# Value product with V stationary in two column halves, and reciprocal sums spread by a product with the identity

## The chip, the cores and the metric

The kernel runs on one core of a Trainium2 chip. The metric is device time in microseconds for one execution, the median of several runs. A core has TensorE (matmul; its weight loads are shown apart), VectorE, ScalarE, GpSimd and the DMA queues, each with its own list of instructions, tied together by semaphores only. In the rows PE is TensorE, PEld its weight loads, DVE VectorE, ACT ScalarE, POOL GpSimd.

## The reference

Two transformer layers on 512 tokens of width 1024. Layer 0 mixes with sliding-window attention (16 query heads, 4 key-value heads, window 128, a learned sink per head), layer 1 with a forgetting attention over all earlier keys. After each comes a router with the same mixture of 16 experts. What the change touches is the attention of both layers:

```python
# layer 0: keys of the block before and of the own block; a sink logit in the softmax
probs = jax.nn.softmax(jnp.concatenate([scores, sink_col], axis=-1), axis=-1)[..., :-1]
out = jnp.einsum('bnhgqs,bnshd->bnqhgd', probs.astype(vv.dtype), vv)
return out.reshape(B, S, SWA_Q_HEADS * HEAD_DIM) @ w_o
# layer 1: all keys up to the own block
p = jax.nn.softmax(jnp.where(causal, s, NEG), axis=-1)
outs.append(jnp.einsum('bhqk,bkhd->bqhd', p.astype(v.dtype), v[:, :end]))
```

Everything is float32. The output projection needs the attention output with the model dimension on partitions, in two parts, attn_high and attn_low, whose sum is the float32 value.

## The kernel before

Layer 0 runs its input projection, then attention, output projection, normalisation, router, experts; layer 1 the same. Attention works on pairs of heads (hp, eight per layer), and for each pair on four blocks of 128 queries in the order 0, 3, 1, 2 (`N_ORDER`). A pair and a block is a step s, 32 steps per layer. In layer 0 block 0 has one key block and the others two; in layer 1 block n has n + 1. So a pair has 7 key blocks in layer 0 and 10 in layer 1.

One step, for both heads ("halves") of the pair:

- TensorE, `scores(s)`: Q times K, two matmuls of 64 rows each, one head in each row half of the array. In layer 1 a bf16 matmul adds the causal mask (L548).
- VectorE, `mask_and_max(s, half)`: bias, and the row's maximum, from PSUM to the buffer sp (L1091 in layer 0, L1098 in layer 1).
- ScalarE, `expo(s, half)`: exponentials and row sums (L807).
- TensorE, `turn_probs(s)`: 128x128 transposes of the probabilities, head 0 to bank 3, head 1 to bank 4 (L559).
- ScalarE copies head 0's from PSUM to the buffer pT (`evac_probs`, L821), VectorE head 1's (L1115). There is one pT for each head, so a copy waits for the product of the step before (pv_done), and the next transposes for the copy.
- TensorE, `mix(s)`: the product with V (L576). Stationary is a 128x128 block of pT, moving are 64 columns of V; the result has queries on partitions. It goes to bank 5 or 6, by the parity of hp, first all of head 0, then all of head 1.

After a pair's four steps VectorE's `normalise(hp)` takes reciprocals of the row sums (L1123 adds the sinks in layer 0, L1126) and divides the bank into heads_out (L1130). TensorE's `turn_out(hp)` turns that into the same bank with four transposes (L584), ScalarE's `out_high_part` casts it to attn_high (L832), and VectorE's `evac_out` makes attn_low (L1137). ScalarE also casts the output weights in the odd steps (L827).

The order on each engine is the order of the code. TensorE's loop is, for each s:

```python
turn_probs(s)
if s >= 1: mix(s - 1)
if s + 2 < STEPS: scores(s + 2)
if s >= NT and s % NT == 1: turn_out(s // NT - 1)
```

VectorE's is copy of step s, masks of step s + 2, then in the first step of the next pair `normalise`, in its third `evac_out`. ScalarE's is exponentials of step s + 1 for head 0, copy of step s, exponentials of step s + 1 for head 1, then the rest. The output projection follows; its matmuls are lines L454 to L456, 21 of them before it needs the last pair.

## Time and profile before

| | us |
|---|---|
| median of 3 runs | 1023.93 (1016.85 to 1025.27) |
| the profiled execution | 1014.57 |
| its span, first to last instruction | 1012.4 |
| layer 0's attention | about 90 to 160 |
| layer 1's attention | about 604 to 691 |
| TensorE busy, share of the span | 879.1, 87% |
| VectorE, ScalarE, GpSimd busy | 385.4, 249.5, 122.5 |

"Busy" is the union of an engine's instructions. Matmuls overlap, so the duration of a row of matmul is longer than its distance to the next row; what counts is the distance from start to start, or the time that the chain of waits gives to a group. A float32 matmul of the code is two rows of MATMUL and two of LDWEIGHTS; a transpose is one. A form such as `64*128` is the part of the array, rows and columns; `128x64` behind it is the size of the moving operand.

### The profile page before, as it was taken

To read this page: it belongs to the slowest core of one execution; us is meant where nothing else is said; L and a number is where in the kernel's file an instruction comes from. 1 tells how busy PE (TensorE), PEld (TensorE's weight loads), DVE (VectorE), ACT (ScalarE), POOL (GpSimd) and SP (SyncE) were. 2 spreads that over 40 slices of the span, in tenths; PEclk is the share of its full clock that TensorE was granted. 3 is DMA by queue.
4 is the path that set the end of the run, shared out by engine and by line. 5 is a ranking of instruction groups with operands and counts; after the bars stand their busy time and mean duration, and the time that the engine had idled before them with its cause. 6 is when DMAs were issued, how large, how long until landed. Compare 5 with 4: busy or idle time off the path is not lost.

```text
span 1012.4 us, 10845 instructions
## 1 busy us (share of the span) xinstructions
PE 879.1 (87%) x3900; PEld 561.4 (55%) x3900; DVE 385.4 (38%) x928; ACT 249.5 (25%) x605; POOL 122.5 (12%) x137
## 2 busy tenths in 40 slices
PE   6999999966899999918999999999975899999910
PEld 5887777852344444306878877877862344444300
DVE  3534884444111111157332226663445111111137
ACT  3323882000121111041222227772000121111100
POOL 2001331113000000032000002221113000000024
PEclk9999999978999999958999999999977899999965
DMA  9996100068699999644162232111059499999234
GB/s 324 339 353 213 48 1 1 1 233 314 178 356 345 351 354 321 213 133 153 63 209 83 84 111 98 43 43 42 1 179 347 135 352 358 351 342 327 93 115 166
DMA packets 110286, 196.69 MB, mean 194 GB/s; under 512 B 6608, under 2 KB 72144, under 8 KB 110240
## 3 DMA queue, kind: packets, MB, share of 16 engines
q1 hardware_dynamic: 92864, 132.34, 38.0%
q0 software_dynamic: 10432, 39.36, 11.6%
q10 hardware_dynamic: 6944, 24.38, 7.4%
q8 instruction: 28, 0.46, 0.2%
q14 instruction: 18, 0.15, 0.0%
HBM read 158.81 MB, written 37.26 MB: 194 GB/s over the span
## 4 chain that ended last, share of the span: by engine, by line
PE 81%; DVE 8%; DMA 4%; POOL 3%; issue 2%; ACT 1%; POOLq 0%; SPq 0%; DVEq 0%; ACTq 0%
PE bank L649 21%; PE bank L661 11%; PE bank L454 10%; PE bank L456 10%; PE bank L455 10%; PE bank L576 5%; PE bank L542 4%; PE bank L559 3%; PE bank L643 2%; PE bank L440 2%; PE bank L611 1%; POOL xs L406 1%; DMA arena<-ys,pos 1%; POOL veps L366 1%; DVE xres L987 1%
## 5 line engine op out<-in xcount | busy, mean ns | idle before, releaser
L649 PE MATMUL bank<-ring,arena 128*96 128x512 f32 x512 | 228.6, 600 | 2.8 <-issue 1.4
L649 PEld LDWEIGHTS bank<-ring,arena 128*96 128x96 f32 x512 | 84.2, 165 | 140.1 <-issue 138.3
L661 PE MATMUL bank<-ring,arena 128*96 128x512 f32 x256 | 116.4, 597 | 2.7 <-DVE arena L1268 2.7
L1268 DVE COPY arena<-bank 128x192 f32<-128x192 f32 x32 | 11.4, 357 | 194.9 <-PE bank L654 194.9
L454 PE MATMUL bank<-high,x_high 128*128 128x512 f32 x160 | 67.1, 419 | 10.5 <-DVE low L993 5.4
L807 ACT ACTIVATE arena<-arena,nmax 128x256 f32<-128x256 f32 (+3 forms) x128 | 66.9, 522 | 31.1 <-DVE nmax L1098 19.9
L661 PEld LDWEIGHTS bank<-ring,arena 128*96 128x96 f32 x256 | 39.1, 162 | 55.3 <-issue 51.1
L576 PE MATMUL bank<-arena 128*128 128x64 f32 x544 | 68.1, 269 | 0.2 <-ACT arena L821 0.2
L576 PEld LDWEIGHTS bank<-arena 128*128 128x128 f32 x544 | 65.8, 192 | 0.5 <-ACT arena L821 0.5
L421 POOL DMA_INDIRECT arena<-ys,pos x16 | 19.5, 1220 | 382.8 <-issue 382.8
L455 PE MATMUL bank<-low,x_high 128*128 128x512 f32 x160 | 65.2, 408 | 0.0
L456 PE MATMUL bank<-high,xlow 128*128 128x512 f32 x160 | 64.8, 405 | 0.0
L393 POOL TENSOR_TENSOR low<-ring,high 128x512 fp32r<-128x512 f32 x32 | 40.6, 1270 | 181.9 <-ACT high L827 181.9
L1278 DVE COPY arena<-bank 96x512 f32<-96x512 f32 x32 | 22.0, 687 | 97.9 <-PE bank L661 97.9
L871 ACT ACTIVATE arena<-bank 96x256 f32<-96x256 f32 x32 | 12.1, 379 | 184.6 <-PE bank L649 184.6
L454 PE MATMUL bank<-high,attn_high 128*128 128x512 f32 x128 | 51.8, 405 | 0.0
L456 PE MATMUL bank<-high,attn_low 128*128 128x512 f32 x128 | 51.2, 400 | 0.0
L455 PE MATMUL bank<-low,attn_high 128*128 128x512 f32 x128 | 51.0, 398 | 0.0
L456 PE MATMUL bank<-x_high,wsplit 128*128 128x512 f32 x128 | 50.6, 395 | 0.0
L454 PE MATMUL bank<-x_high,wsplit 128*128 128x512 f32 x128 | 50.2, 392 | 0.0
L455 PE MATMUL bank<-xlow,wsplit 128*128 128x512 f32 x128 | 49.9, 390 | 0.0
L440 PE MATMUL bank<-ident,xres 128*128 128x128 f32 x128 | 20.8, 316 | 32.1 <-DVE xres L987 27.8
(200 smaller groups left out, 1222.2 us busy)
## 6 DMA issues: line engine op xcount, KB each, us to landing
ring<-in_w_gate SPq DMA_DIRECT2D x32, 1024.0 KB, 7.0
ring<-in_w_up SPq DMA_DIRECT2D x32, 1024.0 KB, 9.6
ring<-in_w_down SPq DMA_DIRECT2D x32, 1024.0 KB, 12.7
ys<-arena ACTq DMA_DIRECT2D x32, 384.0 KB, 6.6
ring<-in_fox_w_in SPq DMA_DIRECT2D x6, 2048.0 KB, 9.3
arena<-xs ACTq DMA_DIRECT2D x30, 384.0 KB, 6.5
xs<-lnp POOLq DMA_DIRECT2D x1, 9984.0 KB, 43.8
ring<-in_swa_w_in SPq DMA_DIRECT2D x3, 2048.0 KB, 12.3
```

The lines of the kernel that those rows point to most:

```text
L393: eng.tensor_tensor(low, w, high, ALU.subtract).then_inc(S(f"out_low{l}"), 1)
L440: mm = eng.transpose(bank[3 + c // 4][:, (c % 4) * P:(c % 4 + 1) * P], xres[:, t, c * P:(c + 1) * P], ident[:, :])
L454: eng.matmul(out, ah, wh, start=(c == 0), stop=False)
L455: eng.matmul(out, ah, wl, start=False, stop=False)
L456: return eng.matmul(out, al, wh, start=False, stop=(c == KC - 1))
L542: mm = eng.matmul(s_bank(s, half)[:, 0:nk], QT[r, hp, n * P:(n + 1) * P], KT[r, kp, k0 * P:k1 * P], start=True, stop=(l == 0))
L559: mm = eng.transpose(bank[3 + half][:, i * P:(i + 1) * P], sp[:, 2 * (s % 2) + half, i * P:(i + 1) * P], ident[:, :])
L576: mm = eng.matmul(bank[5 + hp % 2][:, at:at + HD], pT[:, half, i * P:(i + 1) * P], (V0 if l == 0 else V)[:, k0 + i, v:v + HD], start=(i == ...
L649: mm = eng.matmul(bank[2 + b][0:CAP, :], xeT[:, b, c, :], w[:, c, :], start=(c == 0), stop=(c == KC - 1))
L661: mm = eng.matmul(bank[5 + half][0:CAP, :], hT[:, b, c, :], w[:, c, half * BLK:(half + 1) * BLK], start=(c == 0), stop=(c == FC - 1))
L807: eng.activation(p, p, ACT.Exp, bias=nmax[:, hp % 2, n, half:half + 1], scale=-1.0, accum_out=rsum[:, hp % 2, n, half:half + 1]).then_inc( ...
L1278: eng.tensor_copy(ysb[0:CAP, b, BLK:D], bank[6][0:CAP, :]).then_inc(S(f"y_dve{l}"), 1)
```

## The change

The product is turned round: the 64 columns of V of a head are stationary, 128 columns of pT are moving, and the result has the head's dimension on partitions, already the layout that the output projection wants. Head 0 goes to the left column half of the array and partitions 0 to 63 of bank 5, head 1 to the other half and partitions 64 to 127. The matmuls of the two heads alternate, and both need their pT at the start. The output transposes are gone.

The division now needs the reciprocals along the free dimension: `sums(hp)` on VectorE computes them at the end of the pair's last step, `spread_sums(hp)` on TensorE multiplies them, spread over 64 columns as the stationary operand, with the identity into bank 6 (8 matmuls, 16 rows), `evac_shares(hp)` on ScalarE copies that to heads_out, and `divide(hp)` on VectorE multiplies bank 5 by it. Cast and subtraction then read heads_out in SBUF instead of PSUM. Every pair uses bank 5 for the product and bank 6 for the spread; the first product of a pair waits for o_ready of the pair before, where it waited for aT_ready of two pairs before.

```diff
--- before.py
+++ after.py
@@ -564,25 +564,33 @@
                     hp, n = STEP[s]
                     k0, k1 = keys(n)
                     if s % NT == 0:
-                        if hp >= 2:
-                            eng.wait_ge(S("aT_ready"), PAIRS * l + hp - 1)
+                        if hp >= 1:
+                            eng.wait_ge(S("o_ready"), PAIRS * l + hp)
                         elif l == 0:
-                            eng.wait_ge(S("qkT_free"), GROUPS[0] - 1 + hp)
-                    for half in range(2):
-                        eng.wait_ge(S(f"pT_ready{half}"), STEPS * l + s + 1)
-                        v = HD * (2 * hp // (NH // NKV) if l == 0 else 2 * hp + half)
-                        at = HD * (2 * n + half)
-                        for i in range(k1 - k0):
-                            mm = eng.matmul(bank[5 + hp % 2][:, at:at + HD], pT[:, half, i * P:(i + 1) * P],
-                                            (V0 if l == 0 else V)[:, k0 + i, v:v + HD], start=(i == 0), stop=(i == k1 - k0 - 1))
-                        mm.then_inc(S("pv_done"), 1)
-
-                def turn_out(hp):
-
-                    eng.wait_ge(S("o_ready"), PAIRS * l + hp + 1)
+                            eng.wait_ge(S("qkT_free"), GROUPS[0])
+                    for i in range(k1 - k0):
+                        for half in range(2):
+                            if i == 0:
+                                eng.wait_ge(S(f"pT_ready{half}"), STEPS * l + s + 1)
+                            v = HD * (2 * hp // (NH // NKV) if l == 0 else 2 * hp + half)
+                            mm = eng.matmul(bank[5][HD * half:HD * half + HD, n * P:(n + 1) * P],
+                                            (V0 if l == 0 else V)[:, k0 + i, v:v + HD], pT[:, half, i * P:(i + 1) * P],
+                                            start=(i == 0), stop=(i == k1 - k0 - 1))
+                            if i == k1 - k0 - 1:
+                                mm.then_inc(S("pv_done"), 1)
+
+                def spread_sums(hp):
+
+                    eng.wait_ge(S("sums_ready"), PAIRS * l + hp + 1)
+                    if hp >= 1:
+                        eng.wait_ge(S("shares_here"), PAIRS * l + hp)
                     for n in range(NT):
-                        mm = eng.transpose(bank[5 + hp % 2][:, n * P:(n + 1) * P], heads_out[:, hp % 2, n * P:(n + 1) * P], ident[:, :])
-                    mm.then_inc(S("oT_done"), 1)
+                        for half in range(2):
+                            mm = eng.matmul(bank[6][HD * half:HD * half + HD, n * P:(n + 1) * P],
+                                            rinv[:, hp % 2, n, half:half + 1].to_broadcast([P, HD]), ident[:, :],
+                                            start=True, stop=True)
+                            if n == NT - 1:
+                                mm.then_inc(S("spread"), 1)
 
                 if l == 0:
                     eng.wait_ge(S("consts"), 1)
@@ -594,12 +602,12 @@
                     turn_probs(s)
                     if s >= 1:
                         mix(s - 1)
+                    if s >= NT and s % NT == 0:
+                        spread_sums(s // NT - 1)
                     if s + 2 < STEPS:
                         scores(s + 2)
-                    if s >= NT and s % NT == 1:
-                        turn_out(s // NT - 1)
                 mix(STEPS - 1)
-                turn_out(PAIRS - 1)
+                spread_sums(PAIRS - 1)
 
 
                 def route(t):
@@ -802,7 +810,7 @@
                     nk = P * (min(n, 1) + 1) if l == 0 else P * (n + 1)
                     eng.wait_ge(S("sp_ready"), 2 * STEPS * l + 2 * s + half + 1)
                     if s >= 2 * NT and s % NT == 0 and half == 0:
-                        eng.wait_ge(S("o_ready"), PAIRS * l + hp - 1)
+                        eng.wait_ge(S("sums_ready"), PAIRS * l + hp - 1)
                     p = sp[:, 2 * (s % 2) + half, 0:nk]
                     eng.activation(p, p, ACT.Exp, bias=nmax[:, hp % 2, n, half:half + 1], scale=-1.0,
                                    accum_out=rsum[:, hp % 2, n, half:half + 1]).then_inc(S("exp_done"), 1)
@@ -826,10 +834,17 @@
                     weights_here(eng, OUT_USE[l] + p // KC)
                     eng.copy(high, w).then_inc(S(f"out_high{l}"), 1)
 
+                def evac_shares(hp):
+
+                    eng.wait_ge(S("spread"), 2 * (PAIRS * l + hp + 1))
+                    if hp >= 2:
+                        eng.wait_ge(S("aT_ready"), PAIRS * l + hp - 1)
+                    eng.copy(heads_out[:, hp % 2, :], bank[6][:, :]).then_inc(S("shares_here"), 1)
+
                 def out_high_part(hp):
 
-                    eng.wait_ge(S("oT_done"), PAIRS * l + hp + 1)
-                    eng.copy(attn_high[:, hp, :], bank[5 + hp % 2][:, :]).then_inc(S("aT_high"), 1)
+                    eng.wait_ge(S("o_ready"), PAIRS * l + hp + 1)
+                    eng.copy(attn_high[:, hp, :], heads_out[:, hp % 2, :]).then_inc(S("aT_high"), 1)
 
                 expo(0, 0)
                 expo(0, 1)
@@ -843,8 +858,11 @@
                         expo_sinks(s // NT)
                     if s % 2 == 1:
                         out_weights_high(s // 2)
-                    if s >= NT and s % NT == 2:
+                    if s >= NT and s % NT == 0:
+                        evac_shares(s // NT - 1)
+                    if s >= NT and s % NT == 1:
                         out_high_part(s // NT - 1)
+                evac_shares(PAIRS - 1)
                 out_high_part(PAIRS - 1)
 
                 for t in range(NT):
@@ -1114,7 +1132,7 @@
                         eng.wait_ge(S("pv_done"), 2 * STEPS * l + 2 * (s - 1) + 2)
                     eng.tensor_copy(pT[:, 1, 0:nk], bank[4][:, 0:nk]).then_inc(S("pT_ready1"), 1)
 
-                def normalise(hp):
+                def sums(hp):
 
                     eng.wait_ge(S("exp_done"), 2 * STEPS * l + 2 * NT * (hp + 1))
                     rs = rsum[:, hp % 2, :, :]
@@ -1122,19 +1140,19 @@
                         eng.wait_ge(S("sink_exp"), hp + 1)
                         link(eng.tensor_tensor(esink[:, hp % 2, :, :], esink[:, hp % 2, :, :], rs, ALU.add))
                         rs = esink[:, hp % 2, :, :]
-                    ri = rinv[:, hp % 2, :, :]
-                    link(eng.reciprocal(ri, rs))
-                    eng.wait_ge(S("pv_done"), 2 * STEPS * l + 2 * NT * (hp + 1))
                     if hp >= 2:
-                        eng.wait_ge(S("oT_done"), PAIRS * l + hp - 1)
-                    eng.tensor_tensor(heads_out[:, hp % 2, :].rearrange("p (n h d) -> p n h d", n=NT, h=2),
-                                      bank[5 + hp % 2][:, :].rearrange("p (n h d) -> p n h d", n=NT, h=2),
-                                      ri.unsqueeze(3).to_broadcast([P, NT, 2, HD]), ALU.mult).then_inc(S("o_ready"), 1)
+                        eng.wait_ge(S("spread"), 2 * (PAIRS * l + hp - 1))
+                    eng.reciprocal(rinv[:, hp % 2, :, :], rs).then_inc(S("sums_ready"), 1)
+
+                def divide(hp):
+
+                    eng.wait_ge(S("shares_here"), PAIRS * l + hp + 1)
+                    eng.tensor_tensor(heads_out[:, hp % 2, :], bank[5][:, :], heads_out[:, hp % 2, :], ALU.mult).then_inc(S("o_ready"), 1)
 
                 def evac_out(hp):
 
                     eng.wait_ge(S("aT_high"), PAIRS * l + hp + 1)
-                    eng.tensor_tensor(attn_low[:, hp, :], bank[5 + hp % 2][:, :],
+                    eng.tensor_tensor(attn_low[:, hp, :], heads_out[:, hp % 2, :],
                                       attn_high[:, hp, :], ALU.subtract).then_inc(S("aT_ready"), 1)
 
                 if l == 0:
@@ -1151,11 +1169,13 @@
                             mask_and_max(s + 2, half)
                     if l == 0 and s % NT == 1:
                         shift_sinks(s // NT)
+                    if s % NT == NT - 1:
+                        sums(s // NT)
                     if s >= NT and s % NT == 0:
-                        normalise(s // NT - 1)
+                        divide(s // NT - 1)
                     if s >= NT and s % NT == 2:
                         evac_out(s // NT - 1)
-                normalise(PAIRS - 1)
+                divide(PAIRS - 1)
                 evac_out(PAIRS - 1)
```

On TensorE, at the step in which a pair of layer 0 ends (L576 is the product, L542 scores, L559 transposes of probabilities, L584 the old output transposes, L589 the new product with the identity), before:

```order
L559 MATMUL bank<-ident,arena 128x128 x2
L576 MATMUL bank<-arena 128x64 x4
L542 MATMUL bank<-arena 128x256 x2
L559 MATMUL bank<-ident,arena 128x128 x4
L576 MATMUL bank<-arena 128x64 x2
L542 MATMUL bank<-arena 128x256 x2
L584 MATMUL bank<-ident,arena 128x128 x4
```

and now:

```order
L559 MATMUL bank<-ident,arena 128x128 x2
L576 MATMUL bank<-arena 64x128 x4
L589 MATMUL bank<-ident,rinv 64x128 x8
L542 MATMUL bank<-arena 128x256 x2
L559 MATMUL bank<-ident,arena 128x128 x4
L576 MATMUL bank<-arena 64x128 x2
L542 MATMUL bank<-arena 128x256 x2
```

The spread stands ahead of the scores that VectorE's next masks need, and the product behind the next transposes is the first of the new pair.

On VectorE at the same place (L1115 copies probabilities, L1091 masks, L1123 and L1126 make the reciprocals, L1130 divides; in the new file L1133, L1109, L1141, L1145 and L1150), before:

```order
L1115 COPY arena<-bank 128x128 [waits pv_done,pT_done]
L1091 ISA arena,nmax<-bank,band,sink 128x256 [waits pT_done,s_done]
L1091 ISA nmax 128x1
L1091 ISA arena,nmax<-bank,band,sink 128x256 [waits pT_done,s_done]
L1091 ISA nmax 128x1
L1123 TENSOR_TENSOR esink<-esink,rsum 128x8 [waits sink_exp,exp_done]
L1126 RECIPROCAL rinv<-esink 128x8 [waits dve_step]
L1130 TENSOR_TENSOR arena<-bank,rinv 128x512 [waits oT_done,pv_done,dve_step]
L1115 COPY arena<-bank 128x256 [waits pv_done,pT_done]
```

and now:

```order
L1141 TENSOR_TENSOR esink<-esink,rsum 128x8 [waits sink_exp,exp_done]
L1145 RECIPROCAL rinv<-esink 128x8 [waits spread,dve_step]
L1133 COPY arena<-bank 128x128 [waits pv_done,pT_done]
L1109 ISA arena,nmax<-bank,band,sink 128x256 [waits pT_done,s_done]
L1109 ISA nmax 128x1
L1109 ISA arena,nmax<-bank,band,sink 128x256 [waits pT_done,s_done]
L1109 ISA nmax 128x1
L1150 TENSOR_TENSOR arena<-bank,arena 128x512 [waits shares_here]
L1133 COPY arena<-bank 128x256 [waits pv_done,pT_done]
```

The reciprocals moved ahead of the copy and the masks, one step earlier; the division kept its place behind the masks and now waits for ScalarE's copy.

## Rows read from the trace of the kernel before

**Rows 1.** Stretches: us; busy us of PE, PEld, DVE, ACT, POOL; clock; DMA; GB/s.
```profile
90.00:163.00 73.00, 67.44 (x508) 53.73 (x507) 56.61 (x204) 54.71 (x192) 21.43 (x18) 1.00 0.16 52
605.00:692.00 87.00, 85.81 (x698) 68.92 (x696) 54.18 (x182) 62.66 (x183) 22.92 (x22) 1.00 0.19 61
```

**Rows 2.** Timeline, layer 0's products: start us, us, engine, line, operands, form, rows.
```profile
112.58 1.00 PE L576 MATMUL bank<-arena 128*128 128x64 f32 x8
...
114.50 1.00 PE L576 MATMUL bank<-arena 128*128 128x64 f32 x8
...
116.35 1.00 PE L576 MATMUL bank<-arena 128*128 128x64 f32 x8
...
118.40 0.56 PE L576 MATMUL bank<-arena 128*128 128x64 f32 x4
...
120.94 0.45 PE L576 MATMUL bank<-arena 128*128 128x64 f32 x3
```

**Rows 3.** Chain of waits, one pair of layer 1: start us, us, what.
```profile
622.32 1.73 PE bank L576 x16
...
625.36 0.84 PE bank L576 x8
626.20 1.06 PE bank L542 x4
...
627.70 1.29 PE bank L576 x12
...
630.72 0.39 PE bank L576 x4
...
633.05 1.73 PE bank L576 x16
```

**Rows 4.** Timeline of layer 0, the ring through ScalarE; in brackets idle time and releaser.
```profile
115.15 0.37 ACT L821 COPY arena<-bank 128x256 f32<-128x256 f32 x1
115.42 0.40 ACT L807 ACTIVATE arena<-arena,nmax 128x128 f32<-128x128 f32 x1
...
116.07 0.22 PEld L559 LDWEIGHTS bank<-ident,arena 128*128 128x128 f32 x2 [0.33 <-ACT arena L807]
```

**Rows 5.** Score rows running at 615.5 us: duration ns min/median/max, first and last start.
```profile
L542 PE MATMUL bank<-arena x2: 693/693/693, 615.4 to 615.4; 64*128 64x512 f32 x2
```

**Rows 6.** Timeline of layer 1, from product to scores to the masks' end.
```profile
617.92 0.19 PEld L576 LDWEIGHTS bank<-arena 128*128 128x128 f32 x1
...
618.18 0.30 PEld L542 LDWEIGHTS bank<-arena 64*128 64x128 f32 x4
...
619.78 0.20 DVE L1126 RECIPROCAL rinv<-rsum 128x8 f32<-128x8 f32 x1
```

**Rows 7.** Timeline of TensorE at the forget gate's projection.
```profile
509.04 0.40 PE L456 MATMUL bank<-high,xlow 128*128 128x512 f32 x1
509.27 0.40 PE L454 MATMUL bank<-x_high,wf_parts 128*16 128x512 f32 x1
```

**Rows 8.** Timeline of layer 0 at the end of a pair.
```profile
117.28 0.70 PE L542 MATMUL bank<-arena 64*128 64x256 f32 x4
...
118.83 0.16 DVE L1123 TENSOR_TENSOR esink<-esink,rsum 128x8 f32<-128x8 f32 x1
...
119.26 0.69 DVE L1130 TENSOR_TENSOR arena<-bank,rinv 128x512 f32<-128x512 f32 x1
...
120.01 0.66 PE L584 MATMUL bank<-ident,arena 128*128 128x128 f32 x4 [0.42 <-DVE arena L1130]
```

**Rows 9.** Masks by form: rows, busy us, mean ns of one, idle before.
```profile
L1091 DVE CUSTOM_DVE_ANT_0 arena<-bank,band,sink 128x256 f32<-128x256 f32 x47 | 20.9, 481 | 3.0 <-PE bank L542 1.9
...
L1098 DVE CUSTOM_DVE_ANT_0 arena<-bank,lnp 128x512 f32<-128x512 f32 x16 | 10.4, 689 | 4.9 <-PE bank L548 4.9
```

**Rows 10.** Stretches at the end of layer 1's attention, columns as in the first group.
```profile
690.10:693.50 3.40, 2.38 (x21) 2.11 (x20) 1.36 (x3) 1.00 (x2) 2.29 (x3) 1.00 0.03 5
693.50:696.90 3.40, 3.40 (x11) 2.75 (x9) 0.69 (x1) 0.59 (x1) 0.00 (x1) 0.50 0.92 270
```

## The prediction

> **What bounds the kernel now.** I read the two attention stages, since the change touches nothing else: first the table of stretches, then the timeline and the chain of waits, product by product. In the table [rows 1] layer 0's attention has TensorE busy 67 of 73 us and layer 1's 86 of 87, both at the full granted clock. One pair of heads is four steps, in the order of query blocks 0, 3, 1, 2. From one product of block 3 to the next, layer 0 takes 120.94 - 112.58 = 8.36 us [rows 2] and layer 1 633.05 - 622.32 = 10.73 us [rows 3]. The intervals that begin with the products of blocks 3, 1, 2 and 0 are 1.92, 1.85, 2.05 and 2.54 us in layer 0, and 3.04, 2.34, 3.02 and 2.33 us in layer 1. In layer 1 the chain is TensorE alone, so there fewer TensorE nanoseconds would count. Layer 0 is a ring, and the reader should see in [rows 4] that a transpose waited 0.33 us for ScalarE: a product starts (114.50), ScalarE copies the next step's probabilities for head 0 (115.15) and does the exponentials of the step after it for head 1 (115.42), TensorE transposes those (116.07), and the next product starts (116.35).
>
> **The product itself.** Each product of the code shows as two rows of matmul. Now 16 rows take 1.73 us in the chain, 0.108 us each [rows 3]. Afterwards a row loads 64 columns and streams 128. No row of before has that form. From the scores, full fp32 products too: two rows of 512 columns, one after the other, lie in 1.06 us with their first load, less 0.2 us for load and change of shape, so 0.43 us for 512 columns and 0.107 us for 128 [rows 3]. I take 0.11 us. Whether the two heads run side by side decides the rest. The scores' row halves do: two rows start at 615.4 together and last 693 ns each [rows 5], and four rows of 0.43 us of work take 1.06 us, not 1.7 [rows 3]. I take the same for column halves, since those rows are nearest: 2 x 0.11 us per key block for both heads, 4 x 0.11 now. A pair has 7 key blocks in layer 0 (1.54 us saved) and 10 in layer 1 (2.2 us saved). The other end, no overlap, saves nothing and is kept for the range.
>
> An entry into the halves may cost something. From a full product to the scores, weight loads stand 618.18 - 617.92 = 0.26 us apart [rows 6] where two rows of a product stand 0.11 apart: 0.15 us for that change. But the step from `128*128` to `128*16` costs nothing: 509.04 to 509.27 is the usual 0.23 us of such matmuls [rows 7]. That shape narrows columns, as the new products do, so I take 0.05 us per step (a first load no longer hidden) and keep 0 and 0.15 as ends. The Trainium skill (TensorEngine Tiling, Key Properties) says that changing the tiling mode drains TensorE. The row on `64*128` agrees, the one on `128*16` does not; by the rule alone some 63 further entries would add up to 63 x 0.15 = 9 us, part of it inside the waits below.
>
> **Why layer 0 gains little.** Its ring does not wait for the whole product but for head 0's part, and that is now the first 4 of 8 rows. The new order alternates the heads, so head 0 is done only with the fourth pair: 4 row times again. The 0.65 us from product to ScalarE's copy [rows 4] stay. So the intervals from blocks 1 and 0 become 1.85 and 1.8 us; the one from block 3 becomes 2.2, because the cast to attn_high moves to that step, next to a weight cast on ScalarE.
>
> **The new wait.** All pairs now accumulate in bank 5, so block 0's product of the next pair waits for o_ready, the end of `divide`. From the start of block 2's product, layer 0:
> the product, 4 x 0.11 = 0.44;
> `spread_sums` waits for the reciprocals, which stand on VectorE behind a copy and two masks: after the copy 2 x 0.48 [rows 9], some 0.1 of it overlapped, and 0.4 for sum and reciprocal (118.83 to 119.26 [rows 8]), 1.2 to 1.3 in all, where TensorE needs about 0.8 for transposes and product: 0.4 exposed;
> 16 rows of the product with the identity, in pairs: 8 x 0.11 = 0.88;
> change of shape 0.15, and the scores to the end of the second mask, 117.28 to 118.83 = 1.55 [rows 8];
> `divide`, queued behind those masks, 0.69 [rows 8] and two wakings of 0.04.
> Sum 4.2 us against 2.05. ScalarE's copy of the shares, no longer than the 0.69 of a 512-column pass, lies beside scores and masks and costs nothing; if the division moved ahead of the masks, it would. The four output transposes go, 0.66 us behind 0.42 us of waiting for the old division [rows 8]: that is most of 2.54 - 1.8. The next step's `evac_probs` is queued behind `divide` on VectorE, and ScalarE's waits for the product after it, so nothing fills the hole.
> One pair of layer 0: 2.2 + 1.85 + 4.2 + 1.8 = 10.05 us against 8.36, **+1.7**.
>
> Layer 1, the same walk: product 6 x 0.11 = 0.66; the masks are 512 wide and take 2 x 0.69 [rows 9], so the reciprocals come about 0.7 late; spread 0.88; change 0.15; scores to the end of the second mask, 619.78 - 618.18 = 1.6 [rows 6]; division and wakings 0.77. Sum 4.75 us against 3.02. The other three shrink until ScalarE's ring binds. From block 3: 0.88 until head 0 is done, 0.2 to the copy, 0.3 copy, 0.7 exponentials and read-out, 0.4 transposes, 0.1 waking and entry: 2.6. From blocks 0 and 1, 2.0 each, where TensorE's own transposes and scores of 384 and 512 columns stand. Pair: 11.4 against 10.73, **+0.7**.
>
> At the end of each stage a spread of 0.88 us stands before the output projection, in place of a division of 0.69, its wakings and 0.66 us of transposes [rows 8]: -0.6 each. The copies and the division behind it (about 2.9 us) lie beside 21 matmuls of 0.23 us in the projection's first group (4.9 us).
>
> Sum over seven intervals a layer: 7 x 1.7 - 0.6 + 7 x 0.7 - 0.6 = 11.3 + 4.3 = **+15.6 us**. The profiled execution took 1014.57 us (span 1012.4, and 2.2 around it); the median of the runs shown is 1023.93, 9.4 above it. The sum gives 1030.2 beside the first and 1039.5 beside the second. I predict **1039**.
>
> **The rivals.**
> *The wait is covered, and it is faster* (0.06). Place: block 0's product behind `divide`. If spread to o_ready took no more than TensorE's own scores and transposes (about 1.9 us in layer 1, 1.3 in layer 0), TensorE would bind layer 1: -2.2 for the product, +0.88 - 0.44 for spread against transposes, +0.2 for entries, -1.5 a pair, and layer 0's ring at 1.8 a step gives 7.2 against 8.36. Eight pairs: -12 - 9, 1003. Against it: `divide` stands behind both masks, which gives 2.5 us.
> *Gain and wait balance* (0.16). The reciprocals come in time (0.4 and 0.7 us) and each step's ring runs 0.1 us shorter: -0.8 and -1.1 a pair, -15 in all, 1024.
> *The column halves do not overlap* (0.11), so the change does not do what it says. Then 14 and 20 more row times a pair and 8 more for the spread, at most 2.4 and 3.1 us a pair, 44 in all; some falls into the waits, so about 1072; half an overlap gives 1055. For it speaks that no row here has two column halves.
> *The clock falls* (0.10). Before layer 1's projection TensorE was busy 2.38 of 3.40 us, and the next stretch ran at a granted 0.50, 1.2 GHz [rows 10]; layer 0's stage with 0.92 busy kept 1.00 [rows 1]. The new holes of over 1 us bring layer 0 nearer to the former. A stretch at half clock costs about 1 us; eight to twelve of them give 1050. The Trainium skill (TensorE: Matmul & The Clock Gate, Part 1) calls the throttled state the default that activity releases; the rows agree.
>
> **Numbers.** The forecast has 0.57 and holds 1030 to 1048 by itself (entries at 0 or 0.15 us, reciprocals earlier or later, layer 1's steps 0.1 off). To 0.8 the range takes in most of the balance and the clock, and half an overlap: **1023 to 1062**. 1%, 10 us, is about what a measurement can tell here from no change. Faster by over 1%: 0.06. Within 1%: 0.16 and the lowest tenth of the forecast, 0.21. Slower: 0.73.
>
> **What the new profile would show.** Right: rows that load 64 columns start in twos, 0.11 us between twos; block 0's product waits for VectorE's division, over 1 us in layer 0 and some 0.7 in layer 1; pairs of 10.0 and 11.4 us; a lower busy share of TensorE in both stages; nothing moved elsewhere. Wrong: the division starts before the masks end, or ScalarE's copy of the shares ends last; product rows start one by one; the granted clock leaves 1.00 inside a stage; the spread never waits for the reciprocals.

## The result and the profile after

| | before | after |
|---|---|---|
| median, us | 1021.49 (4 runs, 1016.85 to 1025.27) | 1038.04 (4 runs, 1029.61 to 1038.62) |
| profiled execution, its span, us | 1014.57, 1012.4 | 1029.61, 1027.8 |
| layer 0's attention, first scores to output projection, us | 70.73 | 87.75 |
| layer 1's attention, us | 88.88 | 93.16 |
| product to product, layer 0, intervals from blocks 3, 1, 2, 0, us | 1.93, 1.84, 2.06, 2.53 | 2.29, 1.82, 5.17, 1.82 |
| the same, layer 1, us | 3.03, 2.34, 3.02, 2.34 | 2.69, 2.09, 4.67, 2.03 |

The change made the kernel slower: ratio 1.0145, 95% interval 1.0074 to 1.0216. A pair takes 11.10 us in layer 0 (8.36 before) and 11.48 us in layer 1 (10.73 before). Two of layer 0's pairs have 4.04 and 4.09 us where the others have 5.17; that difference is what the forecast did not have at all. Stage times and intervals here come from the profiled executions, which were 7 and 8 us shorter than the two medians; where those microseconds lie no trace shows.

The table of stretches after answers to [rows 1] (columns as there; the third row is a stretch at the end of layer 0's attention):

```profile
90.00:176.00 86.00, 67.72 (x587) 40.72 (x588) 63.03 (x200) 58.58 (x198) 21.40 (x18) 0.99 0.14 44
620.00:710.00 90.00, 81.95 (x764) 50.76 (x764) 52.44 (x180) 64.39 (x188) 22.18 (x21) 1.00 0.19 60
...
174.00:177.50 3.50, 3.50 (x26) 3.00 (x25) 0.44 (x2) 0.85 (x2) 1.27 (x1) 0.52 0.03 7
```

TensorE is as long busy in layer 0 as before (67.7 against 67.4 us) in a stage that is 17 us longer; in layer 1 it has 8 us of holes in 90, where it had 1.2 in 87. The clock holds but for one stretch of 3.5 us.

The timeline of layer 0 after, over one end of a pair and the beginning of the next, answers to [rows 2, 4, 8]. L1141 adds the sinks, L1145 is the reciprocal, L589 the spread, L1150 the division, L393 GpSimd's subtraction for the low part of the output weights:

```profile
118.25 0.66 PE L576 MATMUL bank<-arena 128*64 128x128 f32 x8
...
120.06 0.66 PE L576 MATMUL bank<-arena 128*64 128x128 f32 x8
...
120.34 1.27 POOL L393 TENSOR_TENSOR low<-ring,high 128x512 fp32r<-128x512 f32 x1 [2.95 <-ACT high L835]
...
120.38 1.25 DVE L1141 TENSOR_TENSOR esink<-esink,rsum 128x8 f32<-128x8 f32 x1
...
121.66 0.20 DVE L1145 RECIPROCAL rinv<-esink 128x8 f32<-128x8 f32 x1
...
121.92 1.09 PE L589 MATMUL bank<-ident,rinv 128*64 128x128 f32 x16 [1.20 <-DVE rinv L1145]
...
122.94 0.70 PE L542 MATMUL bank<-arena 64*128 64x256 f32 x4
...
124.49 0.69 DVE L1150 TENSOR_TENSOR arena<-bank,arena 128x512 f32<-128x512 f32 x1
...
125.23 0.44 PE L576 MATMUL bank<-arena 128*64 128x128 f32 x4 [1.00 <-DVE arena L1150]
...
129.34 0.66 PE L576 MATMUL bank<-arena 128*64 128x128 f32 x8
...
131.20 0.66 PE L576 MATMUL bank<-arena 128*64 128x128 f32 x8
...
131.47 1.30 POOL L393 TENSOR_TENSOR low<-ring,high 128x512 fp32r<-128x512 f32 x1 [2.98 <-ACT high L835]
...
131.47 0.17 DVE L1141 TENSOR_TENSOR esink<-esink,rsum 128x8 f32<-128x8 f32 x1
```

Read it downwards. `[1.20 <-DVE rinv L1145]` means that the engine stood idle for 1.20 us until that instruction of VectorE released it. The last product of the pair starts at 120.06. The sum of eight elements behind the masks, 0.16 us in [rows 8], takes 1.25 us here: it begins 0.04 us after GpSimd's subtraction and ends with it. The spread waits for the reciprocals behind it. The scores come after the spread, the masks after the scores, the division after the masks, and the next product after the division, 5.17 us after the last. At 131.47 the same sum starts together with the subtraction and takes 0.17 us: this is one of the two pairs with 4.1 us.

The chain of waits in layer 1 after, at the same place (answers to [rows 3, 6]):

```profile
644.43 0.13 DVE rinv L1145
...
644.60 1.09 PE bank L589 x16
645.69 0.63 PE bank L542 x4
...
647.30 0.61 DVE arena L1150
...
647.96 0.44 PE bank L576 x4
...
650.06 1.02 PE bank L576 x16
```

The product of 16 rows takes 1.02 us where it took 1.73, and the chain leaves TensorE twice in a pair, for the reciprocals and for the division, where it had been TensorE alone.

What the product and the spread waited for, over the whole program:

```profile
L576 PE MATMUL bank<-arena x544: 272/273/417, 93.3 to 712.1; 128*64 128x128 f32 x182
...
  DVE arena L1150: 24.8, 28
```
```profile
L589 PE MATMUL bank<-ident,rinv x256: 272/273/417, 99.7 to 712.9; 128*64 128x128 f32 x128
...
  DVE rinv L1145: 21.6, 26
```

These sums count TensorE's matmuls and its weight loads apart (28 waits are 14 pairs, each seen twice). The matmuls alone stood 1.00 us a pair for the division in layer 0 and 0.54 in layer 1, and 1.20 us for the reciprocals in the five held pairs of layer 0 and 0.43 in layer 1.

### The profile page after: what moved, and what is told of

It reads as the page before. It is cut to its first block, busy times and chain, and to the rows that moved or that the text cites. A ratio compares the mean times of both kernels' runs of the same rounds, so it can differ in the third digit from the quotient of the medians.

```text
span 1027.8 us, 11268 instructions
## 1 busy us (share of the span) xinstructions
PE 881.2 (86%) x4092; PEld 533.6 (52%) x4092; DVE 392.8 (38%) x928; ACT 258.1 (25%) x621; POOL 122.6 (12%) x137
## 4 chain that ended last, share of the span: by engine, by line
PE 77%; DVE 10%; DMA 4%; issue 3%; POOL 3%; ACT 2%; POOLq 0%; DVEq 0%; SPq 0%
PE bank L657 20%; PE bank L669 11%; PE bank L454 10%; PE bank L456 10%; PE bank L455 10%; PE bank L542 3%; PE bank L576 3%; PE bank L559 2%; PE bank L651 2%; PE bank L589 2%; PE bank L440 2%; PE bank L619 1%; POOL xs L406 1%; DMA arena<-ys,pos 1%; DMA xs<-xres,pos 1%
## 5 line engine op out<-in xcount | busy, mean ns | idle before, releaser
L393 POOL TENSOR_TENSOR low<-ring,high 128x512 fp32r<-128x512 f32 x32 | 40.6, 1272 | 203.2 <-ACT high L835 203.1
L559 PE MATMUL bank<-ident,arena 128*128 128x128 f32 x272 | 50.1, 287 | 5.9 <-ACT arena L829 4.9
L576 PE MATMUL bank<-arena 128*64 128x128 f32 x544 | 44.4, 286 | 11.9 <-DVE arena L1150 10.7
```

The source lines that it names most:

```text
L393: eng.tensor_tensor(low, w, high, ALU.subtract).then_inc(S(f"out_low{l}"), 1)
L559: mm = eng.transpose(bank[3 + half][:, i * P:(i + 1) * P], sp[:, 2 * (s % 2) + half, i * P:(i + 1) * P], ident[:, :])
L576: mm = eng.matmul(bank[5][HD * half:HD * half + HD, n * P:(n + 1) * P], (V0 if l == 0 else V)[:, k0 + i, v:v + HD], pT[:, half, i * P:(i + ...
```

## The experiments

Each ratio, with its 95% interval, is to the kernel before, run beside it (medians 1015.15 to 1016.13 us). The changed kernel was not run again beside them, so its 1038.04 us comes from other runs than theirs; the intervals of the traces compare it more closely. Pairs are read from product to product. Edits are against the changed kernel, unless it says otherwise.

**GpSimd's subtraction in four pieces.** Is VectorE's sum held by the subtraction that runs beside it?

```diff
-eng.tensor_tensor(low, w, high, ALU.subtract).then_inc(...)
+for q in range(4):
+    c = slice(q * P, (q + 1) * P)
+    ins = eng.tensor_tensor(low[:, c], w[:, c], high[:, c], ALU.subtract)
+ins.then_inc(...)
```

> The changed kernel with GpSimd's subtraction of the output weights (L393, 1.27 us) cut into four pieces of 128 columns. Theory (a VectorE instruction with two SBUF inputs stands still while GpSimd works in SBUF): the 1.25 us rows of the sum of sinks and exponentials (L1141, 5 of 8 in layer 0) fall to 0.6 us or less, and the interval from block 2's product to block 0's in layer 0, 5.17 us in five pairs and 4.04 to 4.09 in the rest, is below 4.5 everywhere; layer 0's attention, 87.75 us, loses 4 to 5 us, layer 1's 93.16 stays within 0.5. Rival (the 1.25 us are VectorE's own, or a lock held over all of GpSimd's work): nothing changes. Total 1034 against 1038.

```profile
119.35 1.69 POOL L395 TENSOR_TENSOR low<-ring,high 128x128 fp32r<-128x128 f32 x4 [2.51 <-ACT high L838]
...
119.39 0.43 DVE L1144 TENSOR_TENSOR esink<-esink,rsum 128x8 f32<-128x8 f32 x1
...
123.43 0.44 PE L579 MATMUL bank<-arena 128*64 128x128 f32 x4 [1.00 <-DVE arena L1153]
```

The sum takes 0.43 us, the length of a piece, not of the whole. The interval goes from 5.17 to 4.36 us in the same five pairs, layer 0's attention from 87.75 to 82.63 us, layer 1 stays at 11.48 a pair. The hold is shown, and its length is that of the GpSimd instruction in progress. The total does not show the gain: 1033.72 us, ratio 1.0186 (1.0133 to 1.024), and a profiled span of 1027.7 us against 1027.8, because the two stages of experts, which no edit touches, took 198.3 and 198.6 us in this execution against 195.5 each.

**The two heads in turn** (all matmuls of head 0, then all of head 1). Does the alternating order cost the early release of head 0?

```diff
-for i in range(k1 - k0):
-    for half in range(2):
+for half in range(2):
+    for i in range(k1 - k0):
```

> The changed kernel with the product's rows of head 0 first and then those of head 1, so that the two column halves cannot run side by side. Theory (layer 0 is a ring that waits for head 0's rows only): in layer 0 the intervals from blocks 3, 1 and 0 stay at 2.29, 1.82 and 1.82 within 0.1, that from block 2 grows by about 0.4; layer 1, whose products are longer, loses about 0.3 to 0.9 an interval, some 2 us a pair: 94 grows to about 109. Rival (the saving of the overlap was what carried the change in both layers): each layer-0 interval grows by about 0.4, 1.6 us a pair, 12 us. If the halves did not overlap in the changed kernel either, nothing changes.

```profile
119.95 0.66 PE L576 MATMUL bank<-arena 128*64 128x128 f32 x8
```

Eight rows take the same 0.66 us as in the alternating order: the halves run side by side although the program names them one after the other. Only the product of 16 rows is longer, 1.31 us from first to last start against 0.82. Pairs are 11.1 and 11.6 us (layer 0's first took 13.9, with its sum held for 2.93 us); 1036.17 us in 2 runs, 1.0207 (1.0138 to 1.0276). So the expectation failed: this order does not take the overlap away, and layer 1 lost 0.1 us a pair, not 2. Head 0's last row starts only 13 ns before head 1's, so the order of the code can't win the early release back either.

**The kernel before with one late signal** (an edit of the kernel before: head 0's product signals only when head 1's is done).

```diff
-    mm.then_inc(S("pv_done"), 1)   # after each half
+mm.then_inc(S("pv_done"), 2)       # after both
```

> The kernel before, with one difference: head 0's product does not signal its end; both are signalled with head 1's. Theory (the ring of layer 0 lives on the early signal of head 0): ScalarE's copy comes 4 rows, 0.44 us, later, so the intervals of layer 0 grow from 1.93, 1.84 and 2.06 to about 2.3 each and a pair from 8.36 to about 9.5, +9 us; in layer 1, bound by TensorE, a pair grows from 10.73 by less than 1 us. Rival (TensorE binds layer 0 too): both stages keep their times within 2 us.

```profile
121.40 0.85 PE bank L576 x8
...
122.33 0.38 ACT arena L821
```

ScalarE's copy now follows the end of the product in the chain. Pairs: 8.97 us in layer 0 (+0.61, where about 1.1 was expected) and 11.15 in layer 1 (+0.42); 1025.61 us, 1.0095 (1.005 to 1.0141). The early release of head 0 is real, at 0.6 us a pair in layer 0. In the new form head 0 ends only with the whole product, so a product that is shorter by half releases it no sooner.

**Two banks in turn** for product and spread, as the kernel before had them, so that no product waits for the division of the pair just ended.

```diff
-eng.wait_ge(S("o_ready"), PAIRS * l + hp)          # mix
+eng.wait_ge(S("shares_here"), PAIRS * l + hp)
-... bank[5][HD * half:..., n * P:(n + 1) * P]       # product
+... bank[5 + hp % 2][HD * half:..., n * P:(n + 1) * P]
-... bank[6][HD * half:..., n * P:(n + 1) * P]       # spread, and ScalarE's copy of it
+... bank[6 - hp % 2][HD * half:..., n * P:(n + 1) * P]
-eng.wait_ge(S("shares_here"), PAIRS * l + hp)      # spread
+eng.wait_ge(S("o_ready"), PAIRS * l + hp)
-... bank[5][:, :]                                  # what divide reads
+... bank[5 + hp % 2][:, :]
```

> The changed kernel with the pairs alternating between banks 5 and 6, the spread going to the bank of the next pair; block 0's product then waits for ScalarE's copy of the shares and not for the division. Theory (the new wait of block 0's product on the division, 1.0 us in layer 0 and 0.5 to 0.7 in layer 1): the interval from block 2 to block 0 falls by 1.0 in layer 0 and 0.6 in layer 1, 8 + 5 = 13 us if nothing else takes its place; total about 1026. Rival (VectorE's order holds the ring anyway, since its copy for the next step stands behind the division): the wait moves to the transposes after it and the pair keeps its 10 to 11 us: gain below 4 us.

```profile
643.03 0.13 DVE rinv L1145
...
643.20 1.09 PE bank L589 x16
644.30 0.63 PE bank L542 x4
644.93 0.22 PE bank L548 x2
645.15 0.88 PE bank L559 x8
646.03 0.37 PE bank L576 x4
```

Behind the spread the chain of layer 1 is TensorE alone; the wait for the reciprocals is left. The long interval goes from 4.67 to 4.06 us in layer 1, from 5.17 to 4.09 in layer 0 (2.97 in the pair whose sum is not held). Layer 0's first interval of the kind took 7.28 us: its sum was held for 2.57 us, through two subtractions in a row, and from 100.9 us on TensorE ran for 10.2 us at a granted 0.50. 1021.64 us, 1.0049 (1.0018 to 1.008).

**The division ahead of the masks**, banks as in the change: the other way to free the bank earlier.

```diff
+if s >= NT and s % NT == 0: divide(s // NT - 1)   # now ahead of mask_and_max
-if s >= NT and s % NT == 0: divide(s // NT - 1)   # was behind it
```

> The changed kernel with the division ahead of the two masks on VectorE in the step in which it falls, not behind them. Theory (block 0's product waits for the division behind scores and masks, 2.5 us from the spread's end; ahead of them it would wait 0.2 for the spread's end, 0.6 for ScalarE's copy of the shares, 0.7 for the division, 1.6 in all, while TensorE does scores and transposes in 1.3 and 1.8): the interval from block 2 to block 0 falls by about 0.9 in layer 0 (5.17 to 4.3) and 0.7 in layer 1 (4.67 to 4.0). The masks then come up to 0.8 later, so the intervals behind may give back some 0.2. Rival (ScalarE reaches the copy of the shares only behind its exponentials, and the masks held up hold those): less than 0.3 falls.

Layer 1's interval is 4.06 us, the same as with two banks. In layer 0 it is 4.38, and the one after it grows from 1.82 to 2.16, since the masks now start later: the pair is 10.65 us against 11.10. 1028.37 us, 1.011 (1.0079 to 1.0141). The masks ahead of the division are what the bank's wait is made of, and moving the division only hands part of that wait on in layer 0.

**The reciprocals ahead of the masks**, banks as in the change.

```diff
+if s % NT == NT - 1: sums(s // NT)   # now ahead of mask_and_max(s + 2)
-if s % NT == NT - 1: sums(s // NT)   # was behind it
```

> The changed kernel with the reciprocals of a pair ahead of the two masks of its last step on VectorE, not behind them. Theory (the spread waits for them, 1.2 us in layer 0 where the sum with the sinks stands still behind GpSimd, 0.4 to 0.6 in layer 1): the interval from block 2 to block 0 falls from 5.17 to about 4.0 or less in layer 0 and from 4.67 to about 4.2 in layer 1, since the masks then come 0.4 us later and are hidden behind the spread: 9 + 4 us, total about 1026. Rival (the masks behind them set the division's time, so the wait only moves): the interval from block 2 stays within 0.3 and the total within 4 us of the changed kernel's 1038.

```profile
646.90 0.81 PE bank L576 x12
647.70 0.87 PE bank L589 x16
648.58 0.63 PE bank L542 x4
```

The spread follows the product without a wait. The interval is 4.02 us in layer 1 (-0.65). In layer 0 it is 3.75 in every pair: -0.33 against the undisturbed pairs, and the 1.08 of the hold gone too, because the sum now runs before the subtraction starts. 1018.75 us, 1.0024 (0.9995 to 1.0053): this one move brings the median to where it can't be told from before, though the profiled attention stages (78.86 and 88.59 us) are still 7.8 us longer than before's.

**Both heads in one column half.** The head 1 part goes to the left half too, into bank 6, so the columns that it should fill lie elsewhere, the output is wrong, the router sees other values, and the total (1373.83 us) is not comparable: layer 1's experts took 523 us, where the kernel has an extra loop for tokens beyond an expert's places. Only the attention stages are compared.

```diff
-mm = eng.matmul(bank[5][HD * half:HD * half + HD, n * P:(n + 1) * P],
+mm = eng.matmul(bank[5 + half][0:HD, n * P:(n + 1) * P],
```

> The changed kernel with both heads' products in the left column half (head 1's into bank 6, so its output columns are not the reference's): the row halves of the array stay as they are, only the running side by side is taken away. Theory (side by side is worth one row time of 0.11 us for each two rows, but the ring of layer 0 waits for head 0 only): a 16-row product lasts 1.8 us instead of 1.02, an 8-row product 0.9 instead of 0.59. Rows alternate, so head 0 now ends with the last row but one: intervals of layer 0 grow by 0.4 (blocks 3 and 1) and 0.2 (block 0), a pair by 1.3, 10 us; in layer 1 by 0.2, 0.9, 0.4 and 0.6, a pair by 2.1, 17 us; total about 1065. Rival (the queue already serialises them): nothing changes.

First and last start of the eight rows of one product, in this kernel and then in the changed one (columns as in [rows 5]):

```profile
L576 PE MATMUL bank<-arena x8: 272/273/323, 120.6 to 121.4; 128*64 128x128 f32 x8
```
```profile
L576 PE MATMUL bank<-arena x8: 272/273/323, 120.1 to 120.4; 128*64 128x128 f32 x8
```

Rows stand 109 ns apart one by one (160 ns after the first); in the changed kernel they start in twos, 6 to 7 ns apart, with the same distances from two to two. A pair is 11.3 us in layer 0 (+0.2, where 1.3 was expected) and 12.62 in layer 1 (+1.14, where 2.1 was). The column halves do run side by side. In layer 0 that is worth next to nothing while the waits stand.

**All repairs together**: two banks, reciprocals ahead of the masks, the subtraction in pieces, and the cast to attn_high one step later (`s % NT == 2` where it was `== 1`), away from the weight cast.

> The changed kernel with alternating banks 5 and 6, reciprocals ahead of the masks, GpSimd's subtraction in four pieces, and the cast to attn_high in the pair's third step as before. Theory (all of the loss lies in the new waits and one crowded step of ScalarE): layer 0's intervals from blocks 3, 1, 2, 0 become 1.95, 1.82, 3.2, 1.82, a pair 8.8 against 8.37 before; layer 1's 2.65, 2.1, 3.6, 2.0, a pair 10.35 against 10.73. Attention 75 and 86 us against 70.7 and 88.9 before: total within 3 us of the kernel before. Rival (other waits take their place): pairs above 9.5 and 11 us, total above 1025.

Pairs: 2.04 + 1.82 + 2.68 + 1.83 = 8.36 us in layer 0 and 2.69 + 2.09 + 3.41 + 2.03 = 10.22 us in layer 1, where before had 8.36 and 10.73. 1006.0 us, 0.9895 (0.9845 to 0.9945). The savings add up. In layer 1: 0.61 + 0.65 = 1.26 = 4.67 - 3.41. In layer 0, with the hold of 1.08: 1.08 + 1.08 + 0.33 = 2.49 = 5.17 - 2.68. The attention stages are 69.72 and 84.34 us, 5.5 us less than before; the other 3.6 of the 9.1 us between the two spans lie in stages that were not edited. The interval from block 3 in layer 0 is 2.04 us where the change had 2.29. The cast next to the weight cast was forecast as the cause of the 2.2. Moving it was not tried alone, but each of the other three repairs alone left 2.29 us, and in the changed kernel's first pair, where that step has no cast to attn_high, the interval is 2.04 us: what remains is the cast.

**A second buffer for the probabilities of layer 0** on top of it, so that the copies out of PSUM wait for the product before the last.

```diff
+pT_other = area(8192, 2 * SEQ, "p (b n) -> p b n", b=2)
+def pT_of(l, s): return pT_other if l == 0 and s % 2 else pT
-if s >= 1: eng.wait_ge(S("pv_done"), 2 * STEPS * l + 2 * (s - 1) + 1)
+if s >= back: eng.wait_ge(S("pv_done"), 2 * STEPS * l + 2 * (s - back) + 1)   # back = 2 in layer 0
```

> The combined version with a second buffer for the transposed probabilities in layer 0, so that a copy waits for the product two steps back. Theory (layer 0 is a ring through the single buffer: product, copy, exponentials, transposes): with the ring cut, TensorE's own work binds, about 7.3 us a pair, or ScalarE's, 7.7 to 8; a pair of layer 0 takes 7.8 to 8.2 against 8.8 without, attention 66 to 69 us; layer 1 as in the combined version. Total about 7 us below it and some 5 below the kernel before. Rival (ScalarE's order, exponentials of one head behind the copy of the other, holds the steps): a pair stays above 8.6.

```profile
121.08 0.59 PE bank L583 x8
121.66 0.63 PE bank L549 x4
122.30 0.40 PE bank L566 x2
122.70 0.59 PE bank L583 x8
123.28 0.87 PE bank L596 x16
124.16 0.63 PE bank L549 x4
```

Layer 0's chain is now TensorE alone as well (L583 product, L596 spread). Pair 7.89 us, but for one of 8.90 in which a shift of the sinks was held. 1003.09 us in 4 runs, 0.9866 (0.9817 to 0.9915): the best version, 2.9 us below the one without the buffer where 7 were expected. Its profiled span of 1000.4 us is 12.0 below before's; 8.1 of them lie in the two attention stages.

**The second buffer in the kernel before**, the same edit.

> The kernel before, with the second buffer for the transposed probabilities in layer 0 alone. It shows how much of the best version so far, 1003 us, is the buffer's. Theory (layer 0 of the kernel before is a ring through ScalarE, but TensorE is busy 92% of it): at most the idle 8%, some 0.5 us a pair, and the pair of 8.37 becomes 7.9 to 8.1, since the division before the output transposes stays; layer 1 unchanged at 10.73; total 3 to 4 us below the kernel before, so above the combined versions. Rival (the buffer is what carries the best version): layer 0's attention falls from 70.7 below 67 and the total to 1006 or less.

Pair 8.28 us against 8.36, where 7.9 to 8.1 was expected; 1015.15 us, 0.9967 (0.9927 to 1.0007), no difference that these runs can tell. There the buffer is worth 0.08 us a pair, in the repaired kernel 0.47. The ring through head 0's part binds only the new form.

## Why the prediction was right, and where it was not

The number was 1039, measured 1038.04; the sum was +15.6, the spans differ by 15.4 and the medians by 16.55. The mechanism of the change is as forecast, but the agreement of the totals is in part luck: layer 0's attention grew by 17.0 us, not 11.3, and the rest of the program was 5.9 us shorter where I had 0.

**What bounds layer 0 before**: misread. I called it a ring through ScalarE. The chain of waits there is TensorE alone, but for one stretch a pair through the masks, the reciprocals and the old division:

```profile
117.98 0.38 PE bank L559 x2
...
118.51 0.40 DVE arena L1091
...
119.26 0.70 DVE arena L1130
...
120.01 0.66 PE bank L584 x4
```

The 0.33 us of [rows 4] is a gap of the weight loads; the matmuls beside it have none. Cutting the ring in that kernel gained 0.08 us a pair. The ring stands just behind TensorE there (a signal four rows late cost 0.6 us), and it became the limit with the shorter product, so the intervals of the new kernel came out right all the same.

**The wait for the division**: right. From product to product at the pair's end, term by term, for the first pair of layer 0, whose sum was not held, and for layer 1:

| | forecast | measured |
|---|---|---|
| product start to spread start | 0.84; 1.36 | 0.78; 1.31 |
| spread and change of shape | 1.03; 1.03 | 1.02; 1.02 |
| scores to the masks' end | 1.55; 1.6 | 1.63; 1.68 |
| division and wakings | 0.77; 0.77 | 0.66; 0.66 |
| sum | 4.2; 4.75 | 4.09; 4.67 |

**The other intervals**: 2.2, 1.85 and 1.8 us were forecast for layer 0, and 2.29, 1.82 and 1.82 are there; 2.6, 2.0 and 2.0 for layer 1, and 2.69, 2.09 and 2.03 are there, each within 0.1. (Layer 1's four intervals add up to 11.35, a growth of 0.6 that I rounded to 0.7; 0.75 was measured.)

**The entry into column halves**: too low. From the last row of the transposes to the first of the product 202 ns pass, where rows stand 107 to 109 ns apart: 0.095 us, not 0.05. The Trainium skill (TensorEngine Tiling, Key Properties) says that a change of tiling mode drains TensorE; these rows agree for column halves (no such gap stood between transposes and product before: 109 ns), and the `128*16` row on which I leaned against it was the wrong neighbour. The way out to the scores costs the same 0.095, where I had 0.15, and the two errors cancel.

**The reciprocals' lateness**: 0.4 and 0.7 us forecast, 0.33 and 0.65 measured by moving them.

**The failed step is the term that costs `sum and reciprocal` at 0.4 us in layer 0.** The row it was read from [rows 8] stood in a step where GpSimd was idle. The change moved the sum into the step in which ScalarE's weight cast releases GpSimd's subtraction, and in five pairs of eight it was held for 1.08 us: 5 x 1.08 = 5.4 us of the 17.0, a term that I had at nothing. Four pieces of the subtraction cut it to 0.43 us, and an earlier sum took it away, so the cause is shown. The hold was in the trace of before too, off the path:

```profile
112.12 1.27 POOL L393 TENSOR_TENSOR low<-ring,high 128x512 fp32r<-128x512 f32 x1 [2.71 <-ACT high L827]
...
112.76 0.66 DVE L1105 TENSOR_TENSOR esink<-nmax,sink 128x8 f32<-128x8 f32 x1
```

The shift of the sinks (L1105) started 0.64 us after GpSimd's subtraction and ended with it; it took 0.65 to 0.66 us in six of eight pairs and 0.17 in the other two. The sum itself (L1123) took 0.72 us in the one pair where a subtraction ran beside it. I had read these durations nowhere.

**The ends of the stages**: -0.6 was forecast for each. In layer 1 the seven pairs grew by 5.2 us and the stage by 4.3, so -0.9. In layer 0 five pairs grew by 2.74 us, one by 1.65 and the first by only 0.85 (it had taken 8.91 before, not 8.36), 16.2 in all, and the stage by 17.0, so +0.9. Of that, 1.1 us is the clock: from the product of the last pair's third step to the projection 3.88 us pass, 2.4 of them at a granted 0.50, where the kernels with the same code there and the full clock have 2.74. So without the hold the seven pairs came to 10.8 us against a forecast of 11.9, and the ends made up for it.

**Nothing moved elsewhere**: not quite. Two stages of experts took 195.5 us each where before had 197.4 and 198.0. They lie between 195.5 and 198.6 in all kernels here with a right output, none of which edits them; why they differ from one execution to the next stays open. Layer 1's output projection took 50.30 us against 51.82: it began in before at a half clock [rows 10], and here it does not, as the chain shows:

```profile
712.34 0.87 PE bank L589 x15
713.21 0.43 PE bank L454
713.64 0.23 PE bank L455
713.88 0.23 PE bank L456
```

**The rivals**. *Covered*: no. Its price was 21 us less than before; with the waits really covered (two banks, early reciprocals, a second buffer) 13 us less was measured, 8 of them in the attention stages. *Balance*: the reciprocals were not in time; the kernel in which they are came out level with before. *No overlap*: fallen, rows start in twos. *The clock*: one stretch of 3.5 us at the end of layer 0, for 1.1 us, and none in layer 1, not eight to twelve.

## What to carry to other kernels

Making an operation cheaper on a busy engine pays only as far as that engine binds. Look first at what the cheaper form makes wait: here a bank with one owner, and an operand made late on another engine, turned a pair of layer 1 that could save 0.5 us into one that lost 0.75, and alternating the banks and moving eight numbers' reciprocals ahead of two masks gave it back. When a small operation is moved, price it by what runs on its neighbours in the new place, not by its duration in the old one.

## What the runs showed of the hardware that was not expected

- VectorE's sum of 8 elements with two operands in SBUF took 1.25 us beside a GpSimd subtraction of 1.27 us that had started 0.04 us earlier, 0.43 us beside the same work in four pieces of together 1.69, 2.57 us through two subtractions in a row, and 0.17 us when the two started within 0.01 us of each other. The masks and copies out of PSUM kept their durations beside it (0.69 us for a mask of 512 columns, 0.43 for a copy of 256). Pieces do not always help: early in layer 0 of the best version twelve of them ran in a row for 5.00 us, and a shift of the sinks that began during them stood until the last had ended, 1.63 us. The Trainium skill (SBUF — State Buffer, Who interferes with whom) says that a VectorE instruction with two SBUF inputs contends with a GpSimd instruction that reads SBUF, and that issue order decides which of the two is blocked. The trace agrees for one instruction beside one. What decides whether VectorE gets in between two GpSimd instructions that follow each other (after the first piece in the experiment, only after the last here) no run shows.
- TensorE ran the two column halves side by side even when all of head 0's rows came first in the program (8 rows, first to last start, in 0.39 us either way, against 0.82 with both heads in one half), up to 8 rows; with 16 the order showed (1.31 us against 0.82 in the alternating order).
- From the first row of the product with the identity (16 rows) to the first of the scores behind it 0.97 us pass when TensorE comes to it without a wait, and 1.02 us behind one. The chain of waits gives it 0.87 and 1.09 us; most of that difference is only where the chain begins to count.
